# A two-layer encoder with expert retrieval: scores and first top-16 by segment amid the query products, a second top-16 over 100 sums

## What is computed

```
for l in range(DEPTH):                      # DEPTH = 2, 512 tokens, width 1024
    mod = cond @ w_ada[l] + b_ada[l]        # six vectors of 1024
    sh1, sc1, g1, sh2, sc2, g2 = split(mod, 6)
    h = modulate(rmsnorm(x, norm1_g[l]), sh1, sc1)
    z = h @ w_in[l]
    mix = concat(conv_mixer(z...), pool_mixer(z...)) @ w_out[l]
    x = x + g1 * mix
    h = modulate(rmsnorm(x, norm2_g[l]), sh2, sc2)
    x = x + g2 * peer(h, w_q[l], keys[l], u[l], v[l])

def peer(h, w_q, sub_keys, u_tab, v_tab):   # 8 heads, 2 halves, 128 keys each
    q = h @ w_q                             # 512 x 2048
    s = einsum("thpd,hpkd->thpk", q, sub_keys)
    top_v, top_i = top_k(s, 16)
    comb = top_v[:, :, 0, :, None] + top_v[:, :, 1, None, :]     # 16 x 16 sums
    best_v, best_j = top_k(comb, 16)
    i1 = top_i[:, :, 0][best_j // 16];  i2 = top_i[:, :, 1][best_j % 16]
    gate = softmax(best_v)
    # each token: 128 of the 16384 experts (i1 * 128 + i2)
    y = sum(gate * gelu(u_tab[i] . h) * v_tab[i])
```

## Time and profile before

| | |
|---|---|
| median of 3 runs | 3183.66 us (3183.57 to 3186.3) |
| profiled execution, its own time | 3189.15 us |
| its span, first to last instruction | 3187.3 us |
| PE busy | 3091.1 us (97%) |
| DVE busy | 2457.8 us (77%) |
| ACT busy | 1118.5 us (35%) |
| POOL busy | 1185.7 us (37%) |
| mean traffic over the span | 231 GB/s |

### The profile page before, as it was taken

How to read it: one execution, slowest core, us unless ns; L and a number is a source line. 1 busy time by engine, 2 the same in 40 slices (tenths; PEclk the granted TensorE clock), 3 DMA queues, 4 the chain that set the end, 5 groups by cost and what they waited for, 6 DMA issues and landing times.

```text
span 3187.3 us, 54768 instructions
## 1 busy us (share of the span) xinstructions
PE 3091.1 (97%) x16200; PEld 2682.7 (84%) x16200; DVE 2457.8 (77%) x5952; ACT 1118.5 (35%) x1590; POOL 1185.7 (37%) x765
## 2 busy tenths in 40 slices
PE   6989999999999999999999999999999999999998
PEld 4668888778888899999975788888788889999997
DVE  7981999859995488999977239951799926889987
ACT  3333322234443333333343332223344433333333
POOL 0033445420001366766700334544000024667674
PEclk8999999999999999999999999999999999999999
DMA  6162666445556799999921224444455578999996
GB/s 254 62 216 101 241 231 240 165 139 188 215 207 256 254 362 361 360 361 363 374 91 40 85 82 142 147 145 141 149 218 210 189 287 293 362 358 361 361 371 238
DMA packets 278481, 734.76 MB, mean 231 GB/s; under 512 B 36064, under 2 KB 118368, under 8 KB 276448
## 3 DMA queue, kind: packets, MB, share of 16 engines
q1 hardware_dynamic: 186688, 462.03, 41.7%
q0 software_dynamic: 50688, 151.18, 12.8%
q10 hardware_dynamic: 40992, 120.34, 9.6%
HBM read 613.85 MB, written 119.54 MB: 230 GB/s over the span
## 4 chain that ended last, share of the span: by engine, by line
PE 54%; POOL 18%; issue 14%; DVE 10%; DMA 2%; ACTq 1%; ACT 1%; DVEq 0%; SPq 0%; POOLq 0%
PE bank L507 30%; PE bank L511 15%; POOL z_pad L934 9%; POOL u_pad L928 5%; PE bank L616 3%; POOL z_pad L928 2%; POOL scratch L928 2%; PE bank L528 2%; DVE scratch L1285 2%; PE bank L427 1%; ACTq L826 1%; DVE h L1266 1%; DVE h L1263 1%; PE bank L451 1%; DVE h L1265 1%
## 5 line engine op out<-in xcount | busy, mean ns | idle before, releaser
L507 PE MATMUL bank<-h_hi,w_hi 128*128 128x512 f32 x2528 | 997.9, 395 | 19.2 <-ACT norm_tmp L807 16.3
L673 ACT ACTIVATE w_hi<-ring 128x1024 fp32r<-128x1024 f32 x584 | 615.0, 1053 | 1116.0 <-PE bank L511 1036.8
L507 PE MATMUL bank<-h_lo,w_hi 128*128 128x512 f32 x2528 | 988.2, 391 | 0.0
L913 POOL TENSOR_TENSOR w_lo<-ring,w_hi 128x1024 fp32r<-128x1024 f32 x172 | 442.8, 2575 | 844.2 <-ACT w_hi L673 844.1
L633 PE MATMUL bank<-v_lo,w_hi 128*128 128x368 f32 x2032 | 670.5, 330 | 0.0
L633 PE MATMUL bank<-v_hi,w_hi 128*128 128x368 f32 x2032 | 665.2, 327 | 2.7 <-DVE v_lo L1439 1.8
L511 PE MATMUL bank<-h_hi,w_lo 128*128 128x512 f32 x2528 | 624.3, 389 | 0.0
L507 PEld LDWEIGHTS bank<-h_hi,w_hi 128*128 128x128 f32 x2528 | 476.9, 189 | 119.4 <-ACT w_hi L673 19.1
L507 PEld LDWEIGHTS bank<-h_lo,w_hi 128*128 128x128 f32 x2528 | 476.7, 189 | 97.1
L511 PEld LDWEIGHTS bank<-h_hi,w_lo 128*128 128x128 f32 x2528 | 474.5, 188 | 98.6
L934 POOL DMA_INDIRECT z_pad<-ga_scratch,z_pad x288 | 374.0, 1299 | 155.0 <-issue 86.9
(11 more groups left out here) (184 smaller groups left out, 2885.0 us busy)
## 6 DMA issues: line engine op xcount, KB each, us to landing
ring<-u_t SPq DMA_DIRECT2D x256, 512.0 KB
ring<-v_t SPq DMA_DIRECT2D x256, 512.0 KB
ga_scratch<-norm_tmp ACTq DMA_DIRECT2D x256, 256.0 KB, 2.0
g_scratch<-scratch ACTq DMA_DIRECT2D x12, 4096.0 KB, 13.8
scratch<-ga_scratch SPq DMA_DIRECT2D x256, 192.0 KB
scratch<-ada_t SPq DMA_DIRECT2D x76, 512.0 KB, 5.8
scratch<-g_scratch SPq DMA_DIRECT2D x32, 768.0 KB
keys<-g_scratch SPq DMA_DIRECT2D x32, 768.0 KB
```

The lines of the kernel that those rows point to most:

```text
L507: pe.matmul(to, w_hi[:, b, k * P:(k + 1) * P], part_h[:, k, :], start=(k == 0 and part_h is h_hi), stop=False)
L673: return act.activation(to, of, ACT.Copy)
L913: pool.tensor_tensor(w_lo[:, n % 2, :], ring[:, n % RING, :], w_hi[:, n % 2, :].bitcast(F32), ALU.subtract).then_inc(tile_used[n % RING], 1)
```

## The change

- **Scores by segment.** Behind the query product of chunk n (from 2 on) PE now makes the scores of segment n - 2, four matmuls for the four token blocks, into bank 0 or 1. ACT copies segment n - 3 to `scores` behind its copy of query chunk n. The last three segments follow the last product.
- **First top-16 by pairs of segments.** DVE takes two segments (eight rows of 128 scores) at a time as soon as they are copied, eight times, ahead of the loop over token blocks.
- **100 sums in place of 256.** Ranks 0 to 2 of the first half are combined with all 16 of the second, ranks 3 to 15 with ranks 0 to 3: 48 + 52 candidates. The two ranks of a best pair are worked out from its place by a short chain of small operations.
- **Look-up in half precision.** Both halves are looked up at once: one comparison and one product over 4096 elements in 16 bits, three halving sums (2048, 1024, 512 elements) and two last sums of 128.
- **Modulation.** The eight tiles of layer 0's own g2 leave the query stage and go through `ada_next` ahead of the 48 of layer 1 (now 56 in all; 5, 5 and 4 at three places of each token block). SP issues six `load_next` ahead of each round of four `u` chunks, for eight rounds, beginning with round 1 in place of round 3.
- **Gates 12 chunks sooner.** `RETRIEVING` goes from 56 to 44, so `EARLY` goes from 64 to 52.

```diff
-    NEXT_FROM = 3
-    NEXT_ROUNDS = (N_ADA - NEXT_SLOTS) // RING
+    NEXT_FROM, PER_ROUND = 1, 6
+    OWN_ADA = KC
+    N_NEXT = OWN_ADA + N_ADA
+    NEXT_ROUNDS = (N_NEXT - NEXT_SLOTS) // PER_ROUND
     ADA_FIRST = 2 * KC
-    LATER = N_ADA - ADA_FIRST
+    LATER = N_ADA - ADA_FIRST - OWN_ADA
...
-    RETRIEVING = 14 * N_U // 32
+    RETRIEVING = 11 * N_U // 32
...
     PER_BANK = 512 // P
+    WIDE, NARROW, ROWS_WIDE = 16, 4, 3
...
+
                 def load_next(turn, s):

-                    sp.wait_ge(next_used[s], N_ADA // NEXT_SLOTS * l + turn + 1)
-                    sp.dma_start(ada_next[:, s, :], ada_t[(l + 1) % DEPTH, NEXT_SLOTS * turn + s]).then_inc(next_landed[s], 16)
+                    sp.wait_ge(next_used[s], N_NEXT // NEXT_SLOTS * l + turn + 1)
+                    sp.dma_start(ada_next[:, s, :], ada_t[(l + 1) % DEPTH, NEXT_SLOTS * (turn - 1) + s])\
+                      .then_inc(next_landed[s], 16)
+
+                def load_own(s):
+
+                    sp.wait_ge(next_used[s], N_NEXT // NEXT_SLOTS * l + 1)
+                    sp.dma_start(ada_next[:, s, :], ada_t[l, N_ADA - OWN_ADA + s]).then_inc(next_landed[s], 16)

                 def up_round(r):
                     for s in range(RING):
@@ -354,16 +359,15 @@

                 up_rounds(0, 1)
                 with sp.If(l < LAST):
-                    sp.wait_ge(score_ready, 4 * TT * l + 4 * TT)
+                    sp.wait_ge(score_ready, SEGS * l + SEGS)
                     for s in range(NEXT_SLOTS):
-                        load_next(0 * l, s)
+                        load_own(s)
                     settle(sp)
-                    up_rounds(1, NEXT_FROM)
-                    with sp.Fori(0, NEXT_ROUNDS // 2) as q:
-                        for half in range(2):
-                            for s in range(RING):
-                                load_next(q + 1, RING * half + s)
-                            up_round(2 * q + (NEXT_FROM + half))
+                    with sp.Fori(0, NEXT_ROUNDS // 4) as q:
+                        for half in range(4):
...
@@ -566,22 +570,25 @@
                 mm.then_inc(summed, 1)
                 spread_roots(ROOTS * l + 2)
                 first_two(l, stages["wq"], IN_ORDER, 2 * KC)
+                def score(s):
+
+                    pe.wait_ge(q_ready, N_WQ * l + (s + 1))
+                    if s >= 2:
+                        pe.wait_ge(score_ready, SEGS * l + (s - 1))
+                    for a in range(TT):
+                        mm = pe.matmul(bank[:, s % 2, a * P:(a + 1) * P], q_t[:, s, a * P:(a + 1) * P], keys_v[:, s, :],
+                                       start=True, stop=True)
+                    mm.then_inc(score_product, 1)
+
+                pe.wait_ge(keys_landed, 16 * l + 16)
                 for n in range(2, N_WQ):
                     if n >= 6:

                         pe.wait_ge(q_ready, N_WQ * l + (n - 6 + 1))
                     product(l, 0, stages["wq"] + n, bank[:, 2 + n % 6, :])
-
-                pe.wait_ge(q_ready, N_WQ * l + N_WQ)
-                pe.wait_ge(keys_landed, 16 * l + 16)
-                for a in range(TT):
-                    if a >= 2:
-                        pe.wait_ge(score_ready, 4 * TT * l + 4 * (a - 1))
-                    for s in range(SEGS):
-                        mm = pe.matmul(bank[:, 4 * (a % 2) + s // 4, (s % 4) * P:(s % 4 + 1) * P],
-                                       q_t[:, s, a * P:(a + 1) * P], keys_v[:, s, :], start=True, stop=True)
-                        if s % 4 == 3:
-                            mm.then_inc(score_product, 1)
+                    score(n - 2)
...
@@ -789,16 +796,18 @@
                 root(ROOTS * l + 2)
                 act.wait_ge(coef_ready, 2 * l + 2)
                 shift_hi(2 * l + 1, 3 * KC)
+                def copy_score(s):
+
+                    act.wait_ge(score_product, SEGS * l + (s + 1))
+                    copy(scores[:, :, s, :], bank[:, s % 2, :].rearrange("p (a k) -> p a k", k=P)).then_inc(score_ready, 1)
+
                 for n in range(N_WQ):
                     hi(0, stages["wq"] + n + 2)
                     copy(q_t[:, n, :], bank[:, 2 + n % 6, :]).then_inc(q_ready, 1)
-                for s in range(LATER_SLOTS):
-                    act.wait_ge(later_used[s], LATER // LATER_SLOTS + 1)
-                for a in range(TT):
-                    for b in range(4):
-                        act.wait_ge(score_product, 4 * TT * l + (4 * a + b + 1))
-                        copy(scores[:, a, 4 * b:4 * b + 4, :],
-                             bank[:, 4 * (a % 2) + b, :].rearrange("p (s k) -> p s k", k=P)).then_inc(score_ready, 1)
+                    if n >= 3:
+                        copy_score(n - 3)
+                for s in range(N_WQ - 3, N_WQ):
...
@@ -1240,15 +1249,6 @@
                 gains(1, 4 * KC, COL_NORM2)
                 scale(ROOTS * l + 2, coef[:, 1, :], scaled)
                 lo_h(2 * l + 1, 2 * KC, 3 * KC)
-                with dve.If(l < 1):
-                    for n in range(KC):
...
+                for pair in range(SEGS // 2):
+
+                    def seg(n):
+                        return 2 * pair + n // TT, n % TT
+
+                    dve.wait_ge(score_ready, SEGS * l + (2 * pair + 2))
+                    settle(dve)
+                    top16(PAIR, lambda n: scores[:, seg(n)[1], seg(n)[0], :], lambda n: big_s[:, n, :],
+                          lambda n: vals[:, seg(n)[0], seg(n)[1], :], lambda n: idx_u[:, seg(n)[0], seg(n)[1], :])
...
+                    if nexts[0] - n < OWN_ADA <= nexts[0]:
+                        settle(dve)
+                        with dve.If(l < LAST):
+                            for slot in range(OWN_ADA):
+                                dve.wait_ge(next_used[slot], N_NEXT // NEXT_SLOTS * l + 2)
+                            settle(dve)
+                        add_bias(5 * KC, KC)
...
                 for a in range(TT):
-                    dve.wait_ge(score_ready, 4 * TT * l + 4 * (a + 1))
-                    settle(dve)
-                    sc_a = scores[:, a, :, :]
-                    sc_c = sc_a.rearrange("p s k -> p (s k)").rearrange("p (s k) -> p s k", k=TOPK * TOPK)
-                    top16(SEGS, lambda s: sc_a[:, s, :], lambda s: big_s[:, s, :], lambda s: vals[:, s, :],
-                          lambda s: idx_u[:, s, :])
-                    next_modulation(4 if a < TT - 1 else 3)
-                    link(dve.tensor_tensor(big_4, v2[:, :, 0, :].unsqueeze(3).to_broadcast(shape4),
-                                           v2[:, :, 1, :].unsqueeze(2).to_broadcast(shape4), ALU.add))
...
+                    count(dve.tensor_tensor(big_c[:, :, 0:at].rearrange("p h (i j) -> p h i j", j=WIDE),
+                                            v2[:, :, 0, 0:ROWS_WIDE].unsqueeze(3).to_broadcast(wide),
+                                            v2[:, :, 1, :].unsqueeze(2).to_broadcast(wide), ALU.add))
+                    link(dve.tensor_tensor(big_c[:, :, at:CANDS].rearrange("p h (i j) -> p h i j", j=NARROW),
+                                           v2[:, :, 0, ROWS_WIDE:TOPK].unsqueeze(3).to_broadcast(narrow),
+                                           v2[:, :, 1, 0:NARROW].unsqueeze(2).to_broadcast(narrow), ALU.add))
...
                     top16(HEADS, lambda s: big_c[:, s, :], lambda s: sc_c[:, s, :], lambda s: best[:, s, :],
                           lambda s: bj_v[:, s, :])
-                    next_modulation(3 if a < TT - 1 else 2)
...
+                    next_modulation(5)
+
+                    if a == 0:
+                        dve.wait_ge(score_ready, SEGS * l + SEGS)
+                        count(dve.tensor_copy(iota_rank, iota_b[:, 0:TOPK].unsqueeze(2).to_broadcast([P, TOPK, TOPK])))
                     count(dve.tensor_scalar(ja_u, bj, 4, None, ALU.logical_shift_right))
...
-
...
-                        link(dve.tensor_tensor(eq_4, jf.unsqueeze(3).to_broadcast(shape4),
-                                               iota_f[:, :].unsqueeze(1).unsqueeze(1).to_broadcast(shape4), ALU.is_equal))
-                        link(dve.tensor_tensor(eq_4, eq_4, i2[:, :, half, :].unsqueeze(2).to_broadcast(shape4), ALU.mult))
-                        link(dve.tensor_reduce(to[:, a, :].rearrange("p (h k) -> p h k", k=TOPK), eq_4, AX_X, ALU.add))
-                        next_modulation(3 if a < TT - 1 else 2)
+                    count(dve.tensor_scalar(jb_u, bj, 2, None, ALU.logical_shift_right))
+                    count(dve.tensor_copy(idx_h[:, :, :], idx_u[:, :, a, :]))
+                    count(dve.tensor_copy(j_f, bj))
+                    dve.wait_ge(dve_step, STEPS * l + (FIRST + steps[0] - 2))
...
+                    link(dve.scalar_tensor_tensor(ja_f, jb_f, float(ROWS_WIDE - at // NARROW), ja_f, ALU.add, ALU.max))
...
+                    link(dve.scalar_tensor_tensor(j_at, ja_f, float(WIDE), j_at, ALU.mult, ALU.min))
```

(66 more changed lines are left out.)

61 lines of the change are left out of this document (35 added, 26 removed).

## The result

| | before | changed |
|---|---|---|
| median | 3183.61 us (4 runs) | 3232.36 us (4 runs) |
| ratio, 95% interval | | 1.0152 (1.0134 to 1.0170) |
| span of the profiled execution | 3187.3 us | 3228.6 us |

The change made the kernel slower by 48.8 us. The forecast was 3218, the range 3206 to 3235; rival A, the second starvation in full, had said 3231.

The account below looks back on a forecast made before the run. PE bounds the kernel, busy 3091.1 of 3187.3 us, so its idleness decides. Terms -0.6 + 36.6 - 5.0 + 3.4 = +34.4 us give 3218 beside the median; range 3211 to 3225, with rivals 3206 to 3235.

Parts of the forecast that it names:

- rival A: Layer 0 `u` stage: 16 bits bring nothing, a block lasts 57 us, round 8 waits 12 us; +47, 3231 us; chance 0.22.
- The order of the loads decides: Layer 0, `u` chunk 4: its loads queue behind DVE's sixth modulation product; PE idle 34.4 us, +36.6 with slow restart.
- The stall of chunk 48 goes: Layer 0, `u` chunk 48: PE's wait for chunks queued behind modulation tiles disappears, -5.0 us.
- Scores amid the products: Query stage: 0.91 us a segment between products; `u` chunk 0 begins 0.3 us sooner, -0.6 over both layers.
- The second starvation: Layer 0, chunk 32: round 8's loads wait for block 3's sixth product; +3.4 us, between 0 and 14.
- Slack of the other rounds: Layer 0, rounds other than 8: 5 us to spare or more; round 6's chunk 24 comes at 488, wanted at 491.
- The look-up: DVE's 16-bit look-up: comparison and product 6.9 us, sums 3.3, together 10.2 (7.4 to 13.2), 3.6 less than before.
- B: Layer 0, first wait shorter: lone tile lands faster, look-up at the casts' pace; +25, 3209 us; chance 0.10.
- C: Layer 0: no starvation, the chunk 48 stall goes and nothing comes; -5.6, 3178 us, faster; chance 0.05.
- D: Query stage: each of 13 score segments waits 1 us for its copy; 26 us more, 3244 us; chance 0.03.
- The port's share in the first wait: Ahead of chunk 4: starved PE frees DVE from POOL's port; with 1.68 us a product, wait 4 us longer.
- Gates sooner: Gates 12 chunks earlier, both layers: PE's work behind `EARLY` is the same; cost and gain 0.

Follow-up runs that it names:

- the early tiles alone: Kernel before with its four load_next per round beginning at round 1 in place of round 3, nothing else changed: 3220.85 us, 1.0117.
- second trace of the kernel before: Trace of a repeat run of the kernel before, unchanged: 3184.61 us, 0.9999, span 3184.4 us.

## Why the prediction was right, and where its size was off

- **The order of the loads decides: right.** The sixth product was put at 371.3 and ended at 370.96. PE's first wait was put at 34.4 us and lasted 34.85; that this is so close is in part luck. The landing took 6.7 us and not 7.6, so chunk 4, put at 380.0, began at 378.76, and PE's `u` stage had begun 1.9 us sooner than predicted. With its restart the wait cost 37.0, predicted 36.6. Three runs that change what SP waits for (no product, the fourth, a sooner sixth) moved it to none, 23.8 and 16.3 us, and the early tiles alone slowed the kernel before by 1.2%.
- **The stall of chunk 48 goes: right,** worth 3.4 to 5.0 us.
- **Scores amid the products: right.** The third round of the last query product to that of `u` chunk 0 spans 11.1 us where it spanned 23.1 (304.74 to 327.83), 12.0 less, and 13 periods of 6.35 us in place of 5.44 take 11.8 of it back.
- **The second starvation: the term that was mis-sized.** The sum had +3.4 us for chunk 32 and nothing for other rounds. Measured are 7.7 at chunk 32 and 6.0 at chunks 20 and 24: 13.7, which is 10.3 more. Of the 13.7, 8.4 are idle time, and 5.3 are slow restarts, for which the +3.4 had nothing; only its upper bound of 14 named one. The idle time came from DVE. Its blocks 1 and 2 (starts of L1361 at 387.6, 446.3 and 500.9) took 58.7 and 54.6 us in place of 53.7 each, and the sixth product of block 3 ended at 536.5, put at 529.2. The mean price of 1.68 us a modulation product hid how uneven this is. In block 1 an operation of the rank chain and the product of the look-up met POOL's low parts, 2.42 us for 0.22 and 6.50 for 4.42, and in block 3 the comparison did, 4.41 for 2.29:

```profile
409.36 2.42 DVE L1339 CAST u_pad<-h 128x128 f32<-128x128 uint32 x1
...
415.51 6.50 DVE L1347 TENSOR_TENSOR z_pad<-z_pad,u_pad 128x4096 f16<-128x4096 f16 x1
...
524.26 4.41 DVE L1345 TENSOR_TENSOR z_pad<-u_pad,keys 128x4096 f16<-128x4096 f16 x1
```

- **Slack of the other rounds: wrong.** "5 us to spare or more" does not fit the prediction's own figures for round 6, 488 against 491. The product that round waits for was put at 479 and ended at 486.5.
- **The look-up: right within 0.2 us undisturbed.** 2.29 and 4.42 us make 6.7, predicted 6.9. Undisturbed, the comparison runs at 0.56 ns an element and the product at 1.08, a factor of 1.9. The Trainium skill's "Vector Engine (DVE) Microarchitecture Reference", section 5.1, has two results a cycle for a two-source operation on 16-bit operands that all step by one, and one result for the others; the trace agrees. The prediction had added that by the page's pace the last starvation would go. It grew, for the page prices the operation and not its wait for POOL.
- **Rival A** came out at the measured total, 3231, though not by its mechanism: it needed 16 bits to bring nothing, and the comparison took about half of what that would make it. In B the landing was to be up to 4 us quicker, and it was 0.9 quicker. C and D are out: nothing ran faster, and the periods of the query stage were the 6.35 us of the forecast.
- **The port's share in the first wait.** With 1.68 us a product the prediction would have it 4 us longer; six products at 0.53 more are 3.2. It did not come: the first six products took 1.15 each, since POOL had no low part between 336.6 and 378.2.
- **Gates sooner: 0, right,** twice.

The total was put at +34.4 us: -0.6, +36.6, -5.0 and +3.4. By the second trace of the kernel before, the same terms measured about -0.3, +37.0, -3.4 and +13.7, together +47.0.
